# First two weight tiles loaded and split by halves, and tanh, gated products, turned-probability copies and scalings placed earlier among the splits

## The reference

```python
f = swiglu(rms_norm(h, ffn1_pre_g[l]), ffn1_w_gu[l], ffn1_w_down[l])
h = h + MACARON_SCALE * rms_norm(f, ffn1_post_g[l])
m = hybrid_mixer(rms_norm(h, mix_pre_g[l]), cos, sin, w_in[l], ...)
h = h + rms_norm(m, mix_post_g[l])
```

## Time and profile before

| | us |
|---|---|
| median of 3 runs (1307.13 to 1307.91) | 1307.19 |
| the profiled execution | 1307.46 |
| its span, from the first to the last instruction | 1305.7 |
| TensorE busy | 1296.2 |
| VectorE busy | 896.2 |
| ScalarE busy | 709.0 |

### The profile page before, as it was taken

How to read it: one execution, slowest core, us unless ns; L and a number is a source line. 1 busy time by engine, 2 the same in 40 slices (tenths; PEclk the granted TensorE clock), 3 DMA queues, 4 the chain that set the end, 5 groups by cost and what they waited for, 6 DMA issues and landing times.

```text
span 1305.7 us, 18174 instructions
## 1 busy us (share of the span) xinstructions
PE 1296.2 (99%) x7332; PEld 1102.1 (84%) x7332; DVE 896.2 (69%) x1032; ACT 709.0 (54%) x976; POOL 87.1 (7%) x77
## 2 busy tenths in 40 slices
PE   9999999999999999999999999999999999999999
PEld 7788888987778888888888999888888889998887
DVE  6756556687978755547667567856776766687575
ACT  7544445568746544435766544544467665445451
POOL 0000000000001000000252000000012610000000
PEclk9999999999999999999999999999999999999999
DMA  9866637542376766554665544465656564345562
GB/s 323 270 210 205 204 104 253 166 127 83 130 253 212 263 191 185 187 162 145 190 198 177 175 133 129 143 197 177 195 185 220 172 213 146 105 138 163 176 192 84
DMA packets 64963, 234.42 MB, mean 180 GB/s; under 512 B 7664, under 2 KB 7792, under 8 KB 64752
## 3 DMA queue, kind: packets, MB, share of 16 engines
q1 hardware_dynamic: 62064, 224.42, 53.9%
q10 hardware_dynamic: 2816, 8.84, 1.9%
HBM read 232.19 MB, written 1.05 MB: 179 GB/s over the span
## 4 chain that ended last, share of the span: by engine, by line
PE 90%; DVE 5%; DMA 2%; ACT 2%; issue 1%; POOL 0%; SPq 0%; ACTq 0%; another core or an unknown queue 0%; POOLq 0%; DVEq 0%
PE psum L1923 22%; PE psum L1944 22%; PE psum L1924 22%; PE psum L1929 5%; PE psum L1976 5%; PE psum L1930 5%; PE psum L1991 5%; DMA raw<-weights 2%; PE psum L2124 2%; DVE w_lo L1181 1%; PE psum L2378 1%; DVE y_lo L1181 1%; PE psum L2224 1%; PE psum L2364 0%; ACT y_hi L602 0%
## 5 line engine op out<-in xcount | busy, mean ns | idle before, releaser
L1181 DVE TENSOR_TENSOR w_lo<-raw,w_hi 128x1024 fp32r<-128x1024 f32 x226 | 274.1, 1221 | 136.8 <-ACT w_hi L602 135.3
L602 ACT ACTIVATE w_hi<-raw 128x1024 fp32r<-128x1024 f32 x226 | 237.7, 1056 | 150.7 <-PE psum L1944 115.1
L1181 DVE TENSOR_TENSOR y_lo<-raw,y_hi 128x1024 fp32r<-128x1024 f32 x144 | 175.3, 1221 | 65.9 <-ACT y_hi L602 65.1
L1923 PE MATMUL psum<-w_hi,x_hi 128*128 128x512 f32 x552 | 217.7, 394 | 1.0 <-ACT w_hi L602 1.0
L1924 PE MATMUL psum<-w_hi,x_lo 128*128 128x512 f32 x552 | 214.6, 389 | 0.0
L602 ACT ACTIVATE y_hi<-raw 128x1024 fp32r<-128x1024 f32 x144 | 151.9, 1056 | 84.6 <-PE psum L1944 57.1
L1944 PE MATMUL psum<-w_lo,x_hi 128*128 128x512 f32 x552 | 170.0, 389 | 0.0
L1923 PE MATMUL psum<-y_hi,x_hi 128*128 128x512 f32 (+1 forms) x376 | 148.2, 394 | 0.4 <-DVE arena L1262 0.4
L1924 PE MATMUL psum<-y_hi,x_lo 128*128 128x512 f32 (+1 forms) x376 | 146.3, 389 | 0.0
L1923 PEld LDWEIGHTS psum<-w_hi,x_hi 128*128 128x128 f32 x552 | 103.8, 188 | 23.7 <-issue 3.0
L1944 PEld LDWEIGHTS psum<-w_lo,x_hi 128*128 128x128 f32 x552 | 103.7, 188 | 21.8 <-DVE w_lo L1181 0.4
(11 more groups left out here) (207 smaller groups left out, 2270.5 us busy)
## 6 DMA issues: line engine op xcount, KB each, us to landing
raw<-weights SPq DMA_DIRECT2D x422, 512.0 KB, 4.1
arena<-gains ACTq DMA_DIRECT2D x7, 512.0 KB, 4.9
arena<-gate_bias ACTq DMA_DIRECT2D x2, 1536.0 KB, 7.5
norm<-x_feat SPq DMA_DIRECT2D x4, 256.0 KB, 5.4
res<-x SPq DMA_DIRECT2D x2, 512.0 KB, 8.9
arena<-lru_w ACTq DMA_DIRECT2D x1, 1024.0 KB, 5.4
cst<-consts ACTq DMA_DIRECT2D x1, 736.0 KB, 5.4
out<-res SPq DMA_DIRECT2D x1, 512.0 KB, 2.6
```

The source lines that it names most:

```text
L602: act.activation(slot(t)[0], raw[:, t % RAW, :], ACT.Copy).then_inc(hi_ready, 1)
L1181: dve.tensor_tensor(lo, raw[:, t % RAW, :], hi.bitcast(F32), ALU.subtract).then_inc(lo_ready, 1)
L1923: pe.matmul(out_, l_hi, r_hi, start=start, stop=False, skip_group_check=skip)
```

## The change

- SP loads T0 and T1 in two halves of 512 columns each, with a semaphore for the first halves (`half_loaded`), ACT splits the halves one after the other (`half_hi`, `hi_ready`), DVE makes the low part in one piece as before, and TensorE (`first_gate`) does the high products of both token tiles with the first half, then with the second half, and then all four low products.
- In the first feed-forward, ACT and DVE get an added `refill(base + 1, 1)` and then the first tanh or gated product ahead of the `refill(base + 1)` that was there. In steps 2 and 3 two tiles are refilled ahead of the tanh and the gated product, where it was three.
- In chunks 10 and 11 ACT's `scale_probs` stands ahead of a refill that it stood behind, and in the same stretches DVE's copy of the turned probabilities stands behind one refill of the next chunk's part, where it stood behind three.

```diff
@@ -36,6 +36,7 @@
 LAYERS = 2
 TILE = 1024
 RAW = 4
+HALVED = 2
 BASE_SLOTS = 4
 TAIL_SLOTS = 4
 ROW = 2048
@@ -385,6 +386,8 @@
         x_loaded = [sem(f"x_loaded{i}") for i in range(TOK)]
         feat_loaded = [sem(f"feat_loaded{i}") for i in range(KD // 2)]
         first_gain_loaded = sem("first_gain_loaded")
+        half_loaded = [sem(f"half_loaded{i}") for i in range(HALVED)]
+        half_hi = sem("half_hi")
         ident_loaded = sem("ident_loaded")
         params_loaded = sem("params_loaded")
         small_loaded = sem("small_loaded")
@@ -515,7 +518,11 @@
                     sp.dma_start(first_pair(t), x_feat[t, :, :]).then_inc(feat_loaded[t], 16)
                 if t >= RAW:
                     sp.wait_ge(lo_ready, t - RAW + 1)
-                sp.dma_start(raw[:, t % RAW, :], weights[t, :, :]).then_inc(raw_loaded[t % RAW], 16)
+                if t < HALVED:
+                    sp.dma_start(raw[:, t, 0:TILE // 2], weights[t, :, 0:TILE // 2]).then_inc(half_loaded[t], 16)
+                    sp.dma_start(raw[:, t, TILE // 2:], weights[t, :, TILE // 2:]).then_inc(raw_loaded[t], 16)
+                else:
+                    sp.dma_start(raw[:, t % RAW, :], weights[t, :, :]).then_inc(raw_loaded[t % RAW], 16)
                 if t == 3:
                     for tok in range(TOK):
                         sp.dma_start(res[:, tok, :], x[tok * P:(tok + 1) * P, :]).then_inc(x_loaded[tok], 16)
@@ -598,6 +605,12 @@
 
                 if FREE_AT[t]:
                     act.wait_ge(weights_used, FREE_AT[t])
+                if t < HALVED:
+                    act.wait_ge(half_loaded[t], 16)
+                    act.activation(slot(t)[0][:, 0:TILE // 2], raw[:, t, 0:TILE // 2], ACT.Copy).then_inc(half_hi, 1)
+                    act.wait_ge(raw_loaded[t], 16)
+                    act.activation(slot(t)[0][:, TILE // 2:], raw[:, t, TILE // 2:], ACT.Copy).then_inc(hi_ready, 1)
+                    return
                 act.wait_ge(raw_loaded[t % RAW], 16 * (t // RAW + 1))
                 act.activation(slot(t)[0], raw[:, t % RAW, :], ACT.Copy).then_inc(hi_ready, 1)
 
@@ -696,9 +709,10 @@
                     load_gain(2)
                     load_layer(0)
                     load_pre(3)
+                if f == 0:
+                    refill(base + 1, 1)
+                    swish(0, 0, 0, base)
                 refill(base + 1)
-                if f == 0:
-                    swish(0, 0, 0, base)
                 refill(base + 2)
                 swish(f, 0, 1, base)
                 refill(base + 4)
@@ -723,12 +737,13 @@
                 for i in range(2, FF_STEPS - 1):
                     g = gate_tile(base, i)
                     late = f == 0 and i < 4
-                    for j in range(3 if late else 4):
+                    ahead = 2 if late else 4
+                    for j in range(ahead):
                         refill(g + j)
                     for tok in range(TOK):
                         swish(f, i, tok, base)
-                    if late:
-                        refill(g + 3)
+                    for j in range(ahead, 4):
+                        refill(g + j)
                     refill(g + 4)
                     hidden_copy(f, i, (0, 1))
                     if i < FF_STEPS - 2:
@@ -930,10 +945,11 @@
                 if 0 <= u < len(UNITS1):
                     exps(At(u + 1), rows1[u])
                     sink_part(u)
+                if c in (10, 11):
+                    scale_probs(u)
                 refill(t + 2)
                 if c == 9:
                     heads_copy(1)
-                if UNITS1_BY_DVE <= u < len(UNITS1):
                     scale_probs(u)
                 refill(t + 3)
                 if c in (7, 8):
@@ -1279,9 +1295,10 @@
                     swish_scales(1, 1)
                     refill(base, 2)
                     refill(base, 2)
+                if f == 0:
+                    refill(base + 1, 1)
+                    swiglu(0, 0, (0,))
                 refill(base + 1)
-                if f == 0:
-                    swiglu(0, 0, (0,))
                 refill(base + 2)
                 swiglu(f, 0, (1,))
                 refill(base + 4)
@@ -1546,7 +1564,7 @@
             for c in range(2, MIX_CHUNKS - 2):
                 t = At(MIX_AT + 4 * c)
                 u = c - 6
-                if 0 <= u - 1 < len(UNITS1):
+                if 0 <= u - 1 < len(UNITS1) and c not in (11, 12):
                     probs_copy(At(u), 8)
                 if c == 5:
                     dve.wait_ge(qk_turned, 1)
@@ -1587,6 +1605,8 @@
                 if c in (10, 11):
                     lru_scan(c - 10)
                 refill(t + 1)
+                if c in (10, 11):
+                    probs_copy(At(u + 1), 8)
                 if c == 14:
                     bank_rests(x_lo, x_hi, 0, wide(4, 1024), 0.5, merged_hi, 0, merged_lo)
                 if c == 4:
@@ -2012,6 +2032,25 @@
                 if tok == 0 and q == 3:
                     ins.then_inc(gate_done, 1)
 
+            def first_gate(q):
+
+                pe.wait_ge(half_hi, q + 1)
+                pe.wait_ge(norm_lo, norm_count(0, 0, q))
+                w_hi_, w_lo_ = slot(q)
+                for j in range(2):
+                    if j:
+                        pe.wait_ge(hi_ready, q + 1)
+                    k = 2 * q + j
+                    for tok in range(TOK):
+                        lh = [v[:, k, tok * P:(tok + 1) * P] for v in (x_hi, x_lo)]
+                        high_rows(psum[:, gate_bank(0, tok), :], lh, (w_hi_[:, j * 512:(j + 1) * 512], None), k == 0)
+                pe.wait_ge(lo_ready, q + 1)
+                for tok in range(TOK):
+                    for j in range(2):
+                        ins = pe.matmul(psum[:, gate_bank(0, tok), :], x_hi[:, 2 * q + j, tok * P:(tok + 1) * P],
+                                        w_lo_[:, j * 512:(j + 1) * 512], start=False, stop=False)
+                ins.then_inc(weights_used, 1)
+
             def down(f, i, tok, j):
 
                 last = i == FF_STEPS - 1
@@ -2037,6 +2076,9 @@
                 both = (0, 1)
                 if f == 0:
                     for q in range(4):
+                        if q < HALVED:
+                            first_gate(q)
+                            continue
                         for tok in both:
                             gate(0, 0, tok, q)
                     pe.wait_ge(ident_loaded, 16)
```

## The result

The changed kernel takes 1310.36 us (median of 17 runs, 1308.79 to 1312.62), the kernel before in the same comparison 1307.38 (17 runs, 1306.24 to 1309.54): 3.0 us more, ratio 1.0023 with a 95% interval of 1.0016 to 1.0031. The profiled execution is the slowest of the 17, 1312.62 us with a span of 1310.8; its losses are therefore larger than the median's, and I compare it with the profiled 1307.46 of before first.

The account below looks back on a forecast made before the run. TensorE, busy 99% of the span, bounds the kernel, so only its waits count. Halves and moved splits +1.5, attention -1.1 make +0.4 on 1307.46, 1307.9; the median is 0.27 lower, so 1307.5, range 1304.8 to 1309.2.

Parts of the forecast that it names:

- T14's landing: Step-1 turn: T14 lands about 32.2, TensorE starts about 35.9 instead of 34.31; loss 1.5 us, bounds 0.1 to 2.5.
- Start: First product, with T0 in halves: at 5.8 to 5.9, 1.05 us earlier; bounds 0 and 1.15.
- what is late next: T4 and T5: tanh ahead of T5's split puts TensorE 1.25 us ahead, but T5's low part ends 19.9 instead of 19.2.
- Second half of T4: TensorE in step 0 starts this half at 18.8 instead of 20.06, 1.25 us ahead.
- The two more issues: Loads on SP: two added issues for the halves are hidden, since the loads behind them wait in the queue anyway.
- my bounds of 0 to 0.3 us: Landings up to T7: smaller packets of the halves delay them by 0.1 us, 0 to 0.3.
- T8: Second token tile's tanh waits behind T8; second pair at 24.7 instead of 24.51, the whole 1.3 us given back.
- Attention: Copies near 343 and 362: 1.0 us gained at the first, 1.1 together; bounds 0.2 and 1.9.
- A: Start and first feed-forward: loads of T8 and T14 don't hold up the tanh; 4.1 us gained, 1303.1; chance 0.13.
- B: First 35 us: T14 lands about 3.2 us from issue, loss only 0.1 to 0.3 us; 1306.2; chance 0.13.
- C: Attention gives nothing: the gained 1.0 us becomes a wait for T111's or T115's split; 1308.7; chance 0.07.
- D: Steps 2, 3 and 4: landings stay behind, 1.4 us each; 1311.8, with two steps 1310.4; chance 0.08.

Follow-up runs that it names:

- the kernel with the order alone: Kernel before with only the first feed-forward's moved splits, tanh and gated products, tiles loaded whole: 1311.5 us, ratio 1.0029.
- attention's profile: Profile of the kernel before with only the moved copies and scalings in attention: 1306.74 us, ratio 0.9992.
- the corrected count: Changed kernel with only T5, not T5 and T6, split after step 0's first tanh: 1308.83 us, ratio 1.0006.
- the filling of 8: Changed kernel with 8 unread matmuls of 256 columns on an unused bank ahead of the step-1 turn: 1309.14 us, ratio 1.0009.

## Why the prediction was wrong

I gave 1307.5 us, 1304.8 to 1309.2, and 0.08 to slower by over 0.2%. It is 1310.36, 0.23% slower. Two terms of the sum were wrong: T14's landing was sized too small, and the clock behind the stop was not there at all. The bounds were added up wrongly too: 0.1 lost with 1.9 won gives 1305.4, and 2.5 lost with 0.2 won 1309.5, where I wrote 1305.7 to 1308.9.

- **Start.** 5.8 to 5.9 expected, 6.05 found. The first half landed at least 0.6 us earlier than I had allowed and its split took 0.63 (I had 0.65); the warm-up matmuls took 4.97 us instead of 4.45. 0.9 us instead of 1.05, and worth nothing in the end, as the step on "what is late next" had it (19.51 against 20.06 at T4, and no lead left at 25.46).
- **Second half of T4.** 18.8 expected, 19.51 found: the load of x landed at 14.98, so its square and T4's split behind it came 0.7 us later in this execution (15.01 and 16.29, before 14.33 and 15.59). The two more issues put the issue of this load 1.2 us later (5.70, before 4.54), which I had called hidden. In the nine other profiles with halves the square started at 14.3 to 14.6, within my bounds of 0 to 0.3 us; so most of the 0.7 is this execution's.
- **T8.** Right in kind and size: a wait of 1.37 us (I had 1.5), second pair at 25.46 instead of 24.7, as T8 landed 0.8 us later. That the whole early start is given back there held.
- **T14, a step that failed by its size.** I wrote that T14 "is loaded when T10's low part is done, 27.8 as before", and let it land midway, at 32.2. It landed at 33.8. Neither the start of its load nor the length was worked out for the new order. T6's low part ended at 21.7 (before 21.1), by the late load of x and not by the moved product, since VectorE has two low parts and one gated product ahead of it in either order; the kernel with the order alone has it at 20.8. T10's load began at 21.75 and took 5.35 us (before 4.3), its split ended at 29.45, and T14's load began at 29.47, 1.7 us later than I had it, and took 4.35, by the rows 4.4 (27.8 to 32.2). In the kernel with the order alone T10 came in 4.40 us and T14's load did begin at 27.61; there the load itself took 5.47, landed at 33.08, and the turn was at 36.59. So the landing was late both times, once by its start and once by its length; why these loads take 4.3 us or 5.5 is open. All that follows is late by that: T14's split at 33.91 instead of 32.5, the turn at 37.33 instead of 35.9, and a loss at this place of 3.0 us in the changed kernel, 2.3 with the order alone, instead of 1.5. The runs with T14 ahead or behind show its place to be the cause: 3.1 and 3.8 us, with the clock's part in them. The estimate from the Trainium skill's figures, 3.2 us for 512 KB ("DMA: Bandwidth & Descriptors", on the fixed cost of a DMA), is below all of the loads named here, 3.5 to 6.6 us. The page fitted it on loads that GpSimd issued, and SP issues these.
- **The clock, the step that failed.** No term of the sum had it. I priced the stop by its length alone. Behind it the clock was at the 1.2 GHz level till 43 us: 2.6 us in the profiled execution, 1.8 in the medians. With 1.8 less the change measures 1.2 over before, 1308.6, inside my forecast's own range; the term alone carries the time out of the range. The Trainium skill's page "TensorE: Matmul & The Clock Gate", in "Part 1: The HAM clock gate", says that an idle array goes back to 1.2 GHz. The trace agrees: 0.50 behind this stop. I should have weighed it as soon as my own forecast had a stop of 2.5 us, twice the 1.2 us of any wait in the trace of before, though no run shows what a stop of 2.5 us does.
- **Attention.** 1.1 expected, 1.0 found, alone and in the change, by the profiles, and for the reasons given: the first place frees 1.0 us, at the second VectorE holds TensorE back.
- **Rivals.** A and B are out, T8 and T14 do hold up the tanh. C is out, since both gains of TensorE in attention's profile were kept to the second place. D had the right sign by a wrong way, and that its two steps give 1310.4, the time measured, is luck: no wait of the later steps grew (the step-2 turn, at 56.98, has none), and the landings do not stay behind for good. What it got right is that a late low part is handed on to the load four tiles on, but that acted from T5 to T9 and T13 and from T10 to T14, where I had it start at step 2.

## What to carry to other kernels

Where loads wait for buffers that an in-order engine frees, an instruction put ahead of a split delays the load one buffer ring further on: write down end of split, load, next split anew for every tile up to the wait, and carry no time over "as before". Price a stop of TensorE of some 3 us at its length plus the slower stretch behind it; here that took the median's loss from about 1.2 to 3.0 us, and useless matmuls in the stop were a gain. Before paying for the removal of a wait, look where the next one would stand: here the 1.4 us came back 17 us later.

## What was not expected of the hardware

- The clock fell behind every stop of 3.2 us or more in the profiles (3.22, 3.30, 3.70 and 5.13 us listed), and behind none of 1.0 to 1.8 us; no stop between these was seen. In the same kernel it varied by execution: of the corrected count's 11 runs, with its 3.70 us, 2 had a mean clock of 1.000. For long stops I can't say from which length on it falls. It also fell where no long stop is known: 5 of 33 executions of the kernel before had a mean clock of 0.999 and took 1309.25 to 1310.63 us, though no wait in its profile is over 1.2 us behind the start. Where in them it fell, the record does not say.
- One 512 KB load took between 3.5 and 6.6 us in the same 15 us of the program. Others were under way beside it; that they make the difference is my guess and not shown. A shift of 0.5 us at its issue went with 2.2 us at its landing.
- The warm-up matmuls (12 records) took 4.45 us in before and 4.97 in the changed kernel with nothing changed in them, and 4.25 to 5.47 over all profiles. The same page of the Trainium skill says that the number of slow matmuls at a start differs from run to run. The traces agree by the time alone: 16 such records took 3.61 us in the filling of 8, 0.23 each, against 0.35 to 0.46 here, while the clock's column is 1.00 from the start. The warm-up decides whether a first load that lands 0.6 us earlier is of use.
